# FFN down projection of a two-layer transformer step: a 2x2 block product of seven products in place of eight

## The reference

```
gate, val = split(h @ ffn_w_up)               # h [1024 tokens, 1024], D_FF = 2816
z = silu(dwconv_grid(gate)) * val             # [1024, 2816]
x = x + g2 * (z @ ffn_w_down)                 # ffn_w_down [2816, 1024]
x = rms_norm(x, final_g)
h = rms_norm(x, norm_g_2);  proj = h @ w_in_2 # second layer
```

## Time and profile before

| what | value |
|---|---|
| median of three runs | 2270.85 us |
| span of the profiled execution | 2265.7 us |
| TensorE matmuls busy | 2050.2 us (90%), 15072 instructions |
| TensorE weight loads busy | 1594.0 us (70%) |
| VectorE busy | 1500.4 us (66%) |
| ScalarE busy | 892.1 us (39%) |
| GpSimd busy | 773.6 us (34%) |
| DMA, whole span | 271.16 MB, mean 120 GB/s |
| mean granted TensorE clock | 0.957 of full speed |

### The profile page before, as it was taken

How to read it: one execution, slowest core, us unless ns; L and a number is a source line. 1 busy time by engine, 2 the same in 40 slices (tenths; PEclk the granted TensorE clock), 3 DMA queues, 4 the chain that set the end, 5 groups by cost and what they waited for, 6 DMA issues and landing times. The chain is left out here.

```text
span 2265.7 us, 37012 instructions
## 1 busy us (share of the span) xinstructions
PE 2050.2 (90%) x15072; PEld 1594.0 (70%) x15072; DVE 1500.4 (66%) x2052; ACT 892.1 (39%) x1445; POOL 773.6 (34%) x460
## 2 busy tenths in 40 slices
PE   4989999837878898999999979999899999999898
PEld 1767677636767676788877768887677776776566
DVE  5777767679774548788988870454746676546644
ACT  5453443414434637333333331443434354333320
POOL 1144433300030145877777724533321111111111
PEclk7999999958899999999999999999999999999899
DMA  7535444597655422122221274523211111102512
GB/s 308 182 122 174 151 141 130 154 264 197 167 177 143 159 75 75 56 84 84 84 76 73 84 272 139 177 73 122 85 56 56 66 38 47 66 19 84 195 47 84
DMA packets 181335, 271.16 MB, mean 120 GB/s; under 512 B 74280, under 2 KB 122024, under 8 KB 176816
## 3 DMA queue, kind: packets, MB, share of 16 engines
q1 hardware_dynamic: 164816, 250.57, 33.9%
q10 hardware_dynamic: 16352, 18.22, 2.7%
HBM read 200.53 MB, written 68.23 MB: 119 GB/s over the span
## 5 line engine op out<-in xcount | busy, mean ns | idle before, releaser
L105 PE MATMUL b_ps<-h_hi,b_wpool 128*128 128x512 f32 (+1 forms) x896 | 277.4, 387 | 10.8 <-POOL b_wpool L744 10.8
L2995 PE MATMUL g_ps<-g_h_hi,w 128*128 128x512 f32 x784 | 260.0, 403 | 6.0 <-ACT g_q L3192 5.9
L3313 POOL TENSOR_TENSOR w<-raw_down,w 128x1024 fp32r<-128x1024 f32 x38 | 94.5, 2488 | 464.6 <-ACT w L3168 464.6
L2262 DVE SCALAR_TENSOR_TENSOR e_vars<-grid,vec,e_vars 128x1024 f32<-128x1024 f32 x168 | 216.0, 1285 | 7.4 <-ACT e_vars L2009 4.2
L105 PEld LDWEIGHTS b_ps<-h_hi,b_wpool 128*128 128x128 f32 x896 | 167.8, 192 | 56.3 <-POOL b_wpool L744 14.4
L2995 PEld LDWEIGHTS g_ps<-g_h_hi,w 128*128 128x128 f32 x784 | 149.3, 190 | 40.8 <-ACT g_q L3192 6.9
L105 PE MATMUL b_ps<-h_lo,b_wpool 128*128 128x512 f32 (+1 forms) x448 | 170.6, 381 | 0.0
L2995 PE MATMUL g_ps<-g_h_lo,w 128*128 128x512 f32 x392 | 156.1, 398 | 0.0
L2674 POOL TENSOR_TENSOR g_down_lo<-raw_down,g_down_hi 128x1408 fp32r<-128x1408 f32 x26 | 86.7, 3339 | 142.5 <-ACT g_down_hi L2574 142.5
L2513 PE MATMUL g_pb<-g_z_hi,g_down_hi 128*128 128x512 f32 x286 | 114.8, 401 | 14.7 <-DVE g_down_lo L2751 9.8
L744 POOL TENSOR_TENSOR b_wpool<-raw_in,b_wpool 128x1024 fp32r<-128x1024 f32 x26 | 67.9, 2611 | 173.2 <-ACT b_wpool L530 173.2
(11 more groups left out here) (524 smaller groups left out, 5284.4 us busy)
## 6 DMA issues: line engine op xcount, KB each, us to landing
e_raw_up<-w_ffn SPq DMA_DIRECT2D x22, 1024.0 KB, 4.9
raw_down<-w_down SPq DMA_DIRECT2D x32, 704.0 KB, 4.2
c_op<-ops SPq DMA_DIRECT2D x40, 512.0 KB, 5.0
raw_down<-w SPq DMA_DIRECT2D x38, 512.0 KB, 3.7
raw_in<-w SPq DMA_DIRECT2D x26, 512.0 KB, 4.2
mod_stage<-ada_rows ACTq DMA_DIRECT2D x24, 512.0 KB, 3.7
zs<-e_z SPq DMA_DIRECT2D x21, 512.0 KB, 2.6
ops<-b_xin SPq DMA_DIRECT2D x20, 512.0 KB, 4.7
```

What stands on the lines that cost most here:

```text
L105: last = nc.tensor.matmul(out, w[:, k, :], x[:, k, cols], start=(k == 0 and n == 0), stop=(k == nk - 1 and n == 2))
L2262: STT(out=acc, in0=view, scalar=wt, in1=acc, op0=ALU.mult, op1=ALU.add).then_inc(sem("conv"), 1)
L2995: mm = nc.tensor.matmul(out_bank, ww[w % 2][:, k], xx[g][:, k], start=(k == 0 and a == 0), stop=(k == KD - 1 and a == 2))
L3313: nc.gpsimd.tensor_tensor(w_lo[w % 2], raw[:, w % 2], w_hi[w % 2].bitcast(F32), ALU.subtract).then_inc(sem("lo"), 1)
```

## The change

The down product becomes a 2x2 block product: weights in four blocks (output half x z half: A11, A12, A21, A22, each 4 x 11 tiles), z in four blocks (z half x token half), and seven products of blocks in place of eight. A unit is now one product and one of its four output tiles (`p`), still 33 matmuls; there are 28 units, 924 matmuls. All four units of a product share one right operand. Two of the products use z as it is with weights as they are (P1, P2), the others use sums: three sums of weights per output tile (S1 = A21 + A22, S3 = A11 - A21 and S4 = A12 - S2 are made on GpSimd, S2 = S1 - A11 on VectorE) and four sums of z (on VectorE, `t_sum`). S1 and S2 are stored in scratch memory and loaded again for products P5 and P3. Each product is added to one, two or three of the four blocks of x. The low parts of P2's z are made on GpSimd. There are three weight slots, of which units 3 and on use two.

```diff
+    UNITS = ([(P1, p) for p in range(FOUR)] + [(P2, p) for p in range(FOUR)] + [(x, p) for p in range(FOUR) for x in (P7, P6)]
+             + [(x, p) for x in (P4, P5, P3) for p in range(FOUR)])
+    free_after = {P7: made(P1, FOUR - 1), P6: made(P2, FOUR - 1), P4: made(P7, FOUR - 1), P5: made(P6, FOUR - 1), P3: made(P4, FOUR - 1)}
+    w_slot = lambda n: n if n < 3 else (n + 1) % 2
...
     def sync(sp):
...
+        store_s1(sp, 1)
+        store_s2(sp, 1)
+        sp.wait_ge(sem("s1_stored"), 32)
+        load_tile(sp, ("A22", 2), FOUR + 2, 1)
+        after_low(sp, 10)
+        load_tile(sp, ("A11", 2), 2, 0)
...
+    def z_used(eng, q):
+        o, r = Z[q]
+        if o in (2, 3, 4):
+            eng.wait_ge(sem("t_sum"), NP * (o - 2) + r + 1)
+        else:
+            eng.wait_ge(sem(f"x_lo{o}"), r + 1)
...
     def scalar(act):
+        split_w(act, 5)
+        for r in range(3):
+            split_x(act, P7, r)
+        split_w(act, 6)
+        for r in range(3, NP):
+            split_x(act, P7, r)
+        split_w(act, 7)
...
+        for r in range(NP):
+            split_x(act, P5, r)
+            if r in (1, 4):
+                split_w(act, 18 + r // 4)
+        split_w(act, 20)
+        for i in range(4, 6):
+            squares(act, 0, i)
+        split_w(act, 21)
+        for i in range(6, KD):
+            squares(act, 0, i)
+        for r in range(NP):
+            split_x(act, P3, r)
+            if r == 2:
+                split_w(act, 22)
+        split_w(act, 23)
         for a in range(2):
             root(act, 0, a)
+        after_low(act, 17)
+        split_w(act, 24)
         for k in range(4):
             high(act, 0, k)
+        split_w(act, 25)
         for k in range(4, KD):
             high(act, 0, k)
+        for i in range(3):
+            squares(act, 1, i)
+        split_w(act, 26)
...
     def gpsimd(pool):
+        lo(6)
+        sum_s1(pool, 0)
+        sum_s3(pool, 0)
+        lo(7)
+        lo(8)
+        for p in range(1, FOUR):
+            lo(7 + 2 * p)
+            sum_s1(pool, p)
+            sum_s3(pool, p)
+            lo(8 + 2 * p)
+        for n in range(15, 24):
+            lo(n)
+        sum_s4(pool, 0)
+        lo(24)
+        sum_s4(pool, 1)
+        lo(25)
+        sum_s4(pool, 2)
+        sum_s4(pool, 3)
+        lo(26)
+        lo(27)
...
     def vector(dve):
+        t_sum(dve, P5, 0)
+        t_sum(dve, P5, 1)
+        fold(dve, 0, 3)
+        low_of(P5, 0)
+        t_sum(dve, P5, 2)
+        low_of(P5, 1)
+        add(dve, "c21", P4, 0)
+        t_sum(dve, P5, 3)
+        low_of(P5, 2)
+        t_sum(dve, P5, 4)
...
+        for i in range(4, KD):
+            fold(dve, 0, i)
+        for r in range(NP):
+            low_of(P3, r)
...
         mean(dve, 0)
         norm_out(dve, 0)
+        for p in range(2, FOUR):
+            add(dve, "c22", P5, p)
+            add(dve, "c12", P5, p)
+        add(dve, "c12", P3, 0)
+        for i in range(1, 4):
+            fold(dve, 1, i)
```

More of the change, by code:

```diff
@@ L2413, in ffn_down @@
[L2413 to L2419, removed]
+    FOUR = KD // 2
@@ new lines, in sync @@
+        load_tile(sp, 6, 2, 1)
+        for q in range(Z_T3, Z_T3 + 6):
+            load_z(sp, q)
+        after_low(sp, 4)
+        load_tile(sp, 7, 3, 1)
+        for q in range(Z_T3 + 6, Z_T3 + 8):
+            load_z(sp, q)
+        after_low(sp, 5)
+        load_tile(sp, ("A22", 0), FOUR, 1)
+        for q in range(Z_T3 + 8, Z_T3 + 10):
+            load_z(sp, q)
+        load_x(sp, 0, 2)
+        for q in range(Z_T3 + 10, Z_T2):
+            load_z(sp, q)
+        after_low(sp, 6)
+        load_tile(sp, ("A11", 0), 0, 0)
@@ new lines, in sync @@
+        load_z(sp, Z_T2)
+        load_z(sp, Z_T2 + 1)
+        store_s1(sp, 0)
+        load_x(sp, 1, 2)
+        after_low(sp, 7)
+        load_tile(sp, ("A21", 1), FOUR + 1, 0)
+        for q in range(Z_T2 + 2, Z_T4):
+            load_z(sp, q)
+        store_s2(sp, 0)
+        sp.wait_ge(sem("s1_stored"), 16)
+        load_tile(sp, ("A22", 1), FOUR + 1, 1)
+        after_low(sp, 8)
+        load_tile(sp, ("A11", 1), 1, 0)
+        load_x(sp, 1, 0)
+        load_x(sp, 0, 3)
+        load_x(sp, 1, 3)
@@ L2554, in split_z @@
[L2554 to L2565 removed]
+        for n in range(2):
+            unit_there(pe, n)
@@ L2695, in fold @@
+    def fold(dve, g, i):
+        dve.wait_ge(sem("squares"), g * KD + i + 1)
+        if i > 1:
+            dve.wait_ge(sem("folded"), g * (KD - 1) + i - 1)
         for a in range(2):
@@ L2774, in vector @@
-        add(dve, 1, 2)
+        low_of(P1, 0)
+        low_w(dve, nc.vector, 1)
+        for r in range(1, NP):
+            low_of(P1, r)
+            taps_late(dve, range(r + 2, r + 3))
+        taps_late(dve, range(8, 9))
+        gated_late(dve)
+        add(dve, "c11", P1, 0)
+        add(dve, "c11", P1, 1)
+        t_sum(dve, P7, 0)
+        t_sum(dve, P7, 1)
+        add(dve, "c11", P1, 2)
+        low_of(P7, 0)
+        t_sum(dve, P7, 2)
+        low_of(P7, 1)
+        t_sum(dve, P7, 3)
@@ new lines, in vector @@
+        add(dve, "c11", P1, 3)
+        low_of(P7, 2)
+        add(dve, "c11", P2, 0)
+        t_sum(dve, P7, 4)
+        low_of(P7, 3)
+        t_sum(dve, P7, 5)
+        low_of(P7, 4)
+        add(dve, "c11", P2, 1)
+        t_sum(dve, P6, 0)
+        low_of(P7, 5)
+        t_sum(dve, P6, 1)
+        t_sum(dve, P6, 2)
+        add(dve, "c11", P2, 2)
+        for r in range(3, NP):
+            t_sum(dve, P6, r)
+        sum_s2(dve, 0)
+        add(dve, "c11", P2, 3)
+        for r in range(NP):
+            low_of(P6, r)
@@ new lines, in add_p6 @@
+        def add_p6(p):
+            sum_u2(dve, p)
+            for c in ("c21", "c22", "c12"):
+                add(dve, c, P6, p)
+        for p in range(FOUR):
+            add(dve, "c21", P7, p)
+            add(dve, "c22", P7, p)
+            if p < FOUR - 1:
+                t_sum(dve, P4, 2 * p)
+                sum_s2(dve, p + 1)
+                t_sum(dve, P4, 2 * p + 1)
+                add_p6(p)
+                if p:
+                    fold(dve, 0, p)
+        for r in range(NP):
+            low_of(P4, r)
```

570 lines of the change are left out of this document (367 added, 203 removed).

## The result

| | before | after |
|---|---|---|
| median of the runs | 2267.99 us (4 runs, 2262.39 to 2271.01) | 2330.14 us (4 runs, 2319.3 to 2334.28) |
| ratio | | 1.0275, 95% interval 1.0244 to 1.0306 |
| span of the profiled execution | 2265.7 us | 2329.3 us |
| first to last matmul of `ffn_down` | 255.3 us | 312.7 us |
| what follows the last of these matmuls | 685.9 us | 685.9 us |

The change is slower by 62 us; forecast were 37. The 2330 lie inside the stated range (2273 to 2335), but above the forecast's own 2290 to 2320, and the value nearest to them is the 2324 of the third rival. The stage gives 57.4 of the 63.6 us between the two spans. The other 6.2 lie ahead of it, where the code is the same: the stage starts at 1324.4 before and 1330.6 after, and between 1321.4 and 1333.1 in the traces of the experiments. They are scatter of single executions.

What follows compares the result with a forecast made beforehand. TensorE was taken as the bound outside a few waits, beside a loop over two weight slots. Stage: 216.0 + 72.5 waits + 4 clock = 292.5, 37 longer; 2270.85 + 37 = 2308 us, range 2273 to 2335.

Steps and rivals of the forecast that it cites:

- the third rival: Loads in the stage take two us more on each of eight trips: 2324 us, chance 0.18.
- the walk: Pass through the engines' written orders in `ffn_down` from 1341.94, unit by unit; its new waits sum to 72.5 us.
- units 6 and 7: Their weight splits stand behind P7's pieces on ScalarE, so TensorE waits 3.5 and 7.5 us.
- unit 9: P6's start: VectorE's low parts alternate with GpSimd's instructions under their lock (turns); wait 8 us, bounds 3 and 13.
- units 10 to 15: GpSimd's work and turns, A22's load behind S1's store and S2: waits 4 and 2 at units 12 and 14.
- units 18, 19: P4: weight splits behind P5's pieces, which chain low part, load and sum; waits 3 and 9 us.
- unit 22: P3's splits stand behind folds and squares, its weight split behind z's third piece; wait 7.5 us, bounds 3 and 10.
- end: units 24, 25, 26: Unit 24 is 5.3 late, unit 26 waits behind `norm_out`, adds, fold, squares, split, about 19; waits 28 us in all.
- low clock, start included: Clock falls after six waits, 4 us in all; the first two units at clock 0.66 cost 2.4.
- Loads are slower: Rival: two us more for each of eight load trips (units 6, 7, 12, P5, P3): 2324 us, chance 0.18.
- That only the end chain stays: Rival: the waits ahead of the square sums are absent, only the end's remain: 2261 us, chance 0.10.
- Turns cost little: Rival: VectorE and GpSimd do not alternate under their lock, while loads still cost: 2281 us, chance 0.20.

Runs made afterwards that it cites:

- e6: Changed kernel with e2's order, P5's sums written to a free region so z places free at the sum, unit 19's weight load ahead of four z loads; 2303.99 us.
- e3: Changed kernel with units 6 and 7 first on ScalarE and GpSimd, P1's and P2's adds ahead of P7's sums, S3's load ahead of last z pieces; 2327.82 us.
- e4: Changed kernel with the twelve GpSimd weight sums cut to 128 of 1408 columns, values not the reference's; 2301.02 us.
- e2: Changed kernel with the weight splits of units 18 and 19 and P4's first adds moved earlier; 2329.21 us.
- e5: Changed kernel with z loads, except the first into each place, cut to 64 of 512 columns, values not the reference's; 2309.3 us.
- e7: e6 with e3's order and, at the end, weight splits of units 26 and 27 both ahead of the squares; 2303.46 us.
- e9: e7 with the eight `x3` instructions of the first half moved behind the folds of the second; 2304.27 us.
- e1: Changed kernel with splits and low part of the last units ahead of squares and S4, P5's last adds ahead of `norm_out`; 2323.38 us.
- e11: e9 with e1's order of squares and splits: three squares of the second half ahead of unit 27's weight split; 2301.87 us.
- e8: Changed kernel with the cuts of e4 and e5 together, and z sums of P6, P4 and P5 on 64 of 512 columns; 2269.35 us.

## Why the prediction was right, and where its size was off

The sign held, and so did the mechanism in the main: new waits of TensorE outweigh the 30 us that four units give. 25 us of 62 were missing. They lie ahead of the first square sums: there the walk gives 17.5 + 21 x 7.57 + 44.5 = 221 us, at most 225 with all of its clock, and 244.5 were measured, while the stretch from there to the end of the last unit was forecast at 67.5 and took 68.2. That the time fell inside the range is owed to its upper end, set for slower loads. By its steps, forecast against measured in us:

| step | forecast | after |
|---|---|---|
| 28 units | 212.0 | 212.9 |
| units 6 and 7 | 3.5 + 7.5 = 11 | 11.6 + 2.0 = 13.6 |
| unit 9 | 8 | 7.7 |
| units 10 to 15 | 6 | 9.4 |
| units 18, 19 | 3, 9 | 5.4, 9.4 |
| unit 22 | 7.5 | 7.1 |
| end: units 24, 25, 26 (3.7 is what 28 leaves) | 5.3, 3.7, 19 | 4.5, 1.6, 17.8 |
| other small gaps, the sums among them | 1.7 | 5.9 |
| low clock, start included | 6.4 | 17.6 |
| stage | 292.5 | 312.7 |

*The waits.* 72.5 forecast, 76.5 measured at the places named, 82.4 with all small ones. The end chain was forecast from the end of unit 22: unit 26 at 52.3, last unit's end at 67.5. Measured from 1575.1: 50.1 and 68.2. e6 bears out the chain at units 18 and 19, e3 and e4 the turns at unit 9, e4 the part of the S4 sums in `norm_out` (17.8 to 12.0; the lower bound had 6 for it). Two small slips stand in the walk: its figures for unit 7 give 7.8 and not 7.5, and the 25 us of `norm_out` are those from the end of the roots (9.6), not from 14.6.

*The term that was mis-sized: the clock.* The prediction priced six waits at 4 us in all though its own row gave 1.8 for one of 4.6 us, and though its walk has ten waits of 3 us or more. There are eight waits of 4 to 18 us (units 6, 9, 12, 18, 19, 22, 24, 26), and behind them the matmuls at low clock cost 1.9, 2.1, 1.3, 1.7, 2.5, 1.5, 2.0 and 2.4: 15.4. Eight times 1.8 would have been 14.4. Windows of after, the columns as in the earlier trace rows:

```profile
1384.00:1392.00 8.00, 1.25 (x3) 1.09 (x4) 8.00 (x6) 1.29 (x2) 4.53 (x2) 0.50 0.92 324
1392.00:1400.00 8.00, 8.00 (x29) 6.41 (x29) 8.00 (x6) 2.73 (x3) 4.73 (x2) 0.79 0.86 279
...
1614.00:1622.00 8.00, 0.00 (x0) 0.00 (x0) 6.63 (x11) 2.51 (x3) 0.00 (x0) 0.50 0.71 261
1622.00:1630.00 8.00, 4.75 (x11) 3.79 (x12) 4.93 (x6) 4.65 (x7) 4.15 (x2) 0.50 0.25 69
1630.00:1638.00 8.00, 8.00 (x34) 6.34 (x34) 3.87 (x4) 1.73 (x4) 2.48 (x2) 0.94 0.25 74
```

After a wait the granted clock is 0.50 (1.2 GHz); 29 matmuls fit into 8 us at unit 6, as after the wait of 4.6 us before. A wait of 17.8 us costs 2.4 here and one of 4.6 costs 1.3; in e2, by the same count, it is 1.4 behind 17.8 (unit 26) and 2.6 behind 4.4 (unit 24). The clock is priced by the number of waits, not by their length.

*The step that was missed: when a bank of PSUM comes free.* The walk asked of each unit when its weights and its right operand are there, not when its bank is free. VectorE at unit 6:

```profile
1383.37 2.47 DVE L2941 TENSOR_TENSOR g_turned_rows<-g_v,ahead_of_sq 128x1024 f32<-128x1024 f32 x1 [3.06 <-issue]
...
1386.43 3.52 DVE L2743 TENSOR_TENSOR g_z_hi<-g_turned_rows,g_z_hi 128x1024 fp32r<-128x1024 f32 x1
1389.87 0.74 DVE L2970 SCALAR_TENSOR_TENSOR x<-g_pb,mod,x 128x512 f32<-128x512 f32 x1
```

GpSimd:

```profile
1381.61 3.15 POOL L2763 TENSOR_TENSOR g_down_lo<-raw_down,g_down_hi 128x1408 fp32r<-128x1408 f32 x1 [11.58 <-ACT g_down_hi L2759]
1385.09 3.77 POOL L2884 TENSOR_TENSOR g_beside_rows<-g_down_extra,g_beside_rows 128x1408 f32<-128x1408 f32 x1 [0.33 <-DMA g_beside_rows<-w_down]
```

Unit 6's weights are ready at 1384.8, 5.1 after the end of unit 5 (1379.65); the forecast had 3.5. The bank comes free only with the `add` that ends at 1390.6, and that stands in VectorE's order behind P7's sum 3 (L2941) and a low part. The sum starts at 1383.37 because the second of its z loads, issued at 1375.80, lands at 1383.29, 7.5 us later where the walk took 4.2; then it waits for low part 6 on GpSimd, and the low part behind it for S1. The turn with S1 is the small part: in e4 that low part takes 1.21 in place of 3.52, and unit 6 still waits 11.0, as sum 3 again waits for its load (landed at 1380.39, sum at 1380.47). With short z loads (e5) unit 6 waits 1.5, but unit 7 6.9. So it was an order behind a slow load, and the third rival has its share here. The bank wait swallowed most of unit 7's forecast wait, so the two together are 2.6 off.

*The rivals.* "Loads are slower" came nearest in time (2324). That only the end chain stays is refuted (six other waits of 4 us or more). "Turns cost little" is refuted by 12.73 for four low parts (12.77 in e3). "Loads are slower" holds in part: 5.7 us is the median landing where 4.2 was taken, unit 6's were 6.6 to 7.5, and e5 shows 21 us for short z loads, which bounds what the z loads cost in all, not what they cost beyond 4.2. At the places that the walk named, its waits sum to only 4 us less than measured. By the ledger the missing 25 us are clock (11), smaller waits (8), the matmuls' pitch (1) and, ahead of the stage or within the noise of the medians, 5.

*Where the four units went.* Before, nine units stood between the two square sums; now there are five. TensorE's own work there fell from 75.3 to 45.1 us (five units 37.9, sums 1.7, 24 matmuls 5.5), yet sums to sums fell only from 81.8 to 73.8. e2, e3, e5 and e6 leave the order behind the first sums as it is and have 72.8 to 73.8, so they say only that what comes ahead doesn't matter there. Four orders of this stretch were tried with the full work: e7 and e9 have 72.7 and 73.1, e1 and e11 69.4 and 71.2. Roots, eight normalised pieces with low parts, `x3`, eight squares and seven folds make a chain on VectorE and ScalarE that nine units covered and five do not; the sums S4 lengthen it through the lock (64.4 in e4). No order tried got under 69 with the full work, and with the cuts of e8 it is still 63 to 66. That the chain itself could be rebuilt (folds on TensorE, say) was not tried and stays open.

## What to carry to other kernels

Before taking matmuls out of a stage, measure the chains that run beside it between two fixed points; taking out 30 us of TensorE where 82 us hold a chain of some 70 gave back 8 to 12 in the five orders tried. Price each new wait twice, its length and some 2 us of low clock behind it. Walk every unit through all its releases: weights, right operand, and the bank or slot that another in-order engine frees. A wait that is mended by order alone mostly turned up one or two units later (those of units 6, 18 and 26 did); the one that went for good took a freed buffer and an earlier load.
